# The new tokens' down product: four full-precision matmuls of 32 columns side by side, summed at the end

## What is computed

```python
D_MODEL = 1024; SEQ = 2048; DEC_SEQ = 32; D_FF = 4 * D_MODEL

def merge_and_ffn(x, oa, ob, oc, gc, onorm_c, w_o, norm_ffn, w_up, w_down):
    ...
    mixed = jnp.concatenate([...], axis=-1)
    h = x + jnp.einsum('bte,ed->btd', mixed, w_o)
    u = jax.nn.relu(jnp.einsum('btd,df->btf', rmsnorm(h, norm_ffn), w_up))
    return h + jnp.einsum('btf,fd->btd', u * u, w_down)
```

## Time and profile before

| what | value |
|---|---|
| median of 3 executions | 3143.09 us (3139.33 to 3143.40) |
| the profiled execution | 3146.91 us, of which its span (first to last instruction) 3145.2 us |
| PE busy | 2971.3 us, 94% of the span |
| DVE, ACT, POOL busy | 1645.0, 960.7, 327.9 us |
| DMA | 310 MB moved, mean 99 GB/s |
[...]
| last third of the MLP | about 2722 to 3145 us of the span |

### The profile page before, as it was taken

How to read it: one execution, slowest core, us unless ns; L and a number is a source line. 1 busy time by engine, 2 the same in 40 slices (tenths; PEclk the granted TensorE clock), 3 DMA queues, 4 the chain that set the end, 5 groups by cost and what they waited for, 6 DMA issues and landing times.

```text
span 3145.2 us, 45442 instructions
## 1 busy us (share of the span) xinstructions
PE 2971.3 (94%) x18200; PEld 2624.4 (83%) x18200; DVE 1645.0 (52%) x2241; ACT 960.7 (31%) x1621; POOL 327.9 (10%) x504
## 2 busy tenths in 40 slices
PE   6999789989999999869999999999999999999999
PEld 4678678878888899857899999888999998888887
DVE  4545244357556578863545445535544545455554
ACT  3322155545555322112322212223221222322221
POOL 1222110011000144640000000000000000000000
PEclk9999899999999999989999999999999999999999
DMA  6652322246222544323211212232121212232221
GB/s 208 191 194 99 104 79 77 71 138 175 70 85 75 160 133 145 108 92 121 94 54 62 72 54 88 89 105 81 65 70 54 81 67 109 83 108 81 81 81 42
DMA packets 280227, 310.23 MB, mean 99 GB/s; under 512 B 53036, under 2 KB 233870, under 8 KB 280018
## 3 DMA queue, kind: packets, MB, share of 16 engines
q1 hardware_dynamic: 280018, 307.33, 30.0%
HBM read 239.51 MB, written 67.78 MB: 98 GB/s over the span
## 4 chain that ended last, share of the span: by engine, by line
PE 52%; DMA 1%; DVE 1%; ACT 1%; issue 0%; SPq 0%; ACTq 0%; DVEq 0%
PE mf_psO L2058 28%; PE mf_psT L2099 22%; PE mf_psO L2099 1%; PE mf_psO L2081 1%; DMA mf_nat<-scratch_mix 1%; PE mf_psT L2044 1%; DVE mf_wlo L1945 1%; ACT mf_whi L1874 1%; DVE mf_acc L2015 0%; ACT mf_hs L1927 0%; DVE mf_acc L1968 0%; DVE mf_hs L1974 0%; SPq L1819 0%; ACT mf_xhi L1889 0%; SPq L1850 0%
## 5 line engine op out<-in xcount | busy, mean ns | idle before, releaser
L2015 DVE TENSOR_TENSOR mf_acc<-mf_psO,mf_acc 128x1024 f32<-128x1024 f32 x272 | 332.8, 1224 | 381.9 <-PE mf_psO L2058 381.6
L2099 PE MATMUL mf_psT<-mf_xhi,mf_wlo 128*128 128x384 f32 (+1 forms) x1440 | 459.3, 319 | 0.0
L2099 PE MATMUL mf_psT<-mf_xhi,mf_whi 128*128 128x384 f32 (+1 forms) x1440 | 459.2, 319 | 0.0
L2099 PE MATMUL mf_psT<-mf_xlo,mf_whi 128*128 128x384 f32 (+1 forms) x1440 | 459.2, 319 | 0.0
L2058 PE MATMUL mf_psO<-mf_whi,mf_uhi 128*128 128x512 f32 (+1 forms) x1088 | 429.1, 394 | 9.2 <-DVE mf_acc L2015 9.2
L2058 PE MATMUL mf_psO<-mf_wlo,mf_uhi 128*128 128x512 f32 (+1 forms) x1088 | 427.4, 393 | 0.0
L2058 PE MATMUL mf_psO<-mf_whi,mf_ulo 128*128 128x512 f32 (+1 forms) x1088 | 427.3, 393 | 0.0
L1874 ACT ACTIVATE mf_whi<-mf_st 128x2048 fp32r<-128x2048 f32 x108 | 206.1, 1911 | 555.3 <-PE mf_psO L2058 528.9
L2099 PEld LDWEIGHTS mf_psT<-mf_xhi,mf_whi 128*128 128x128 f32 x1440 | 270.4, 188 | 2.8
L2099 PEld LDWEIGHTS mf_psT<-mf_xlo,mf_whi 128*128 128x128 f32 x1440 | 270.3, 188 | 1.7
L2099 PEld LDWEIGHTS mf_psT<-mf_xhi,mf_wlo 128*128 128x128 f32 x1440 | 270.4, 188 | 0.0
(11 more groups left out here) (199 smaller groups left out, 5459.7 us busy)
## 6 DMA issues: line engine op xcount, KB each, us to landing
mf_st<-in_w_up SPq DMA_DIRECT2D x48, 1024.0 KB, 5.4
mf_st<-in_w_down SPq DMA_DIRECT2D x48, 1024.0 KB, 6.2
md_wst<-in_w_in SPq DMA_DIRECT2D x24, 1024.0 KB, 5.3
pj_wst<-in_w_in SPq DMA_DIRECT2D x18, 1024.0 KB, 6.7
scratch_proj<-pj_ob SPq DMA_DIRECT2D x48, 256.0 KB, 2.0
mf_st<-in_w_o SPq DMA_DIRECT2D x12, 1024.0 KB, 6.1
pj_xin<-in_x_prompt SPq DMA_DIRECT2D x16, 512.0 KB, 5.6
md_qn<-scratch_proj SPq DMA_DIRECT2D x64, 128.0 KB, 2.7
```

The costliest lines, as they stand in the source:

```text
L2015: nc.vector.tensor_tensor(acc[0:r, i, :], psO[k % 2][0:r, :], acc[0:r, i, :], ALU.add).then_inc(s["o_out"], 1)
L2099: last = nc.tensor.matmul(up_psum(t, f, b, cn), wa[b4][:, w0:w0 + P], xa[:, j, c0:c0 + cn], start=j == 0 and q == 0, stop=j == KD - 1 and ...
```

## The change

It concerns the new tokens' down product in the last third (`t == LAST`), and nothing in the first two thirds.

- **PE.** For each piece the 12 float32r matmuls of the new tokens are replaced by `new_tokens`: four matmuls on plain float32 operands, g = 0 to 3, one for each pair of hidden block and half of the output columns. Each has 32 columns of weights (the squared activations, `mf_usq`) and 512 moving columns (the unsplit weights), and writes to PSUM partitions 32g to 32g+31, so each lies in its own quarter of PE's columns. Each starts and stops its own sum, nothing is accumulated in PSUM.
- **Order.** In the last third the new tokens' product comes first in each piece, not last (`order_of`), on PE and on DVE.
- **DVE.** It copies the last 32 columns of `sq` to `usq` (one copy for each hidden block, between the square and its low part); it adds the product's 128x512 to `mf_part` in place of the add of 32x1024 to `acc`. After the last piece two adds of 32x1024 bring the four quarters into `acc` (the new tokens' rows).
- **SP.** Each w_down piece of the last third is loaded twice: unsplit into both halves of `mf_nat` (p even) or `mf_xin` (p odd), and into `mf_st` as before. The unsplit load comes first and waits for the new tokens' product of p-2 (for p = 0 and 1: for the last use of the tile before). At the end `mf_part` is moved to `mf_hs` in four DMAs of 64 KB, quarter to the new tokens' rows, before the stores; the new tokens' store comes last, after the two adds.
- **Tiles.** `nat`, `xin` and `hs` become one tile each with two halves.

```diff
+        wraw = [nat2, xin2]
+        usq = S.sb("mf_usq", [P, 2 * FP, NEW])
+        part = S.sb("mf_part", [P, 512])
+        def order_of(t, p):
+            n = len(THIRDS[t])
+            return [n - 1, *range(n - 1)] if t == LAST and p >= 0 else list(range(n))
...
             def load_piece(t, what, p):
                 m = piece(t, what, p)
+                src = piece_src(what, p)
+                if t == LAST and what == "d":
+                    if p >= 2:
+                        sp.wait_ge(s["o_done"], o_index(t, 0, p - 2) + 1)
+                    elif p == 0:
+                        sp.wait_ge(s["t_ready"], t_index(t, len(THIRDS[t]) - 1, False) + 1)
+                    else:
+                        sp.wait_ge(s["o_out"], o_index(t, len(THIRDS[t]) - 1, -1) + 1)
+                    sp.dma_start(wraw[p % 2][:, :, :], src).then_inc(raw_loaded[p % 2], 16)
                 if m >= 2:
...
+                    if t == LAST and i == 0:
+                        sp.wait_ge(s["o_out"], o_index(t, 0, NP - 1) + 1)
+                        for g in range(4):
+                            sp.dma_start(hs2[0:NEW, g // 2, (g % 2) * 512:(g % 2) * 512 + 512],
+                                         part[g * NEW:(g + 1) * NEW, :]).then_inc(gathered, 16)
...
+            sp.wait_ge(parts_ready, 2)
+            sp.dma_start(y(t0, r), acc[0:r, len(THIRDS[LAST]) - 1, :]).then_inc(stored, 16)
...
+                        if t == LAST and b == 1:
+                            if f >= 2 * FP:
+                                dve.wait_ge(s["o_done"], o_index(t, 0, f // FP - 2) + 1)
+                            nc.vector.tensor_copy(usq[:, f % (2 * FP), :], sq[k % 2][:, cn - NEW:cn]
+                                                  ).then_inc(usq_ready, 1)
                         dve.wait_ge(s["uhi_ready"], k + 1)
...
+                            if t == LAST and i == nt - 1:
+                                if p == 0:
+                                    nc.vector.tensor_copy(part[:, :], psO[k % 2][:, 0:512]).then_inc(s["o_out"], 1)
+                                else:
+                                    nc.vector.tensor_tensor(part[:, :], psO[k % 2][:, 0:512], part[:, :],
+                                                            ALU.add).then_inc(s["o_out"], 1)
+                                continue
...
+            dve.wait_ge(gathered, 16 * len(TILES[1::2]) + 64)
+            mine = acc[0:NEW, len(THIRDS[LAST]) - 1, :]
+            for j in range(2):
+                if j:
+                    dve.wait_ge(parts_ready, j)
+                nc.vector.tensor_tensor(mine, mine, hs2[0:NEW, j, :], ALU.add).then_inc(parts_ready, 1)
...
+                def new_tokens(k, p):
+                    pe.wait_ge(s["o_out"], k - 1)
+                    pe.wait_ge(usq_ready, FP * (p + 1))
+                    pe.wait_ge(raw_loaded[p % 2], RAW0 + 16 * (p // 2 + 1))
+                    for g in range(4):
+                        j, half = divmod(g, 2)
+                        last = nc.tensor.matmul(psO[k % 2][g * NEW:(g + 1) * NEW, 0:512],
+                                                usq[:, (FP * p + j) % (2 * FP), :],
+                                                wraw[p % 2][:, j, half * 512:half * 512 + 512], start=True, stop=True)
                     last.then_inc(s["o_done"], 1)
```

More of the change, by code:

```diff
@@ L1698, in merge_and_ffn @@
         mhalf = S.sb("mf_mhalf", [P, 1])
-        nat = [S.sb(f"mf_nat{i}", [P, D]) for i in range(2)]
-        xin = [S.sb(f"mf_xin{i}", [P, D]) for i in range(2)]
-        hs = [S.sb(f"mf_hs{i}", [P, D]) for i in range(2)]
+        nat2, xin2, hs2 = [S.sb(z, [P, 2, D]) for z in ("mf_nat", "mf_xin", "mf_hs")]
+        nat, xin, hs = [[z[:, i, :] for i in range(2)] for z in (nat2, xin2, hs2)]
         ss = S.sb("mf_ss", [P, len(TILES)])
@@ L1711, in merge_and_ffn @@
         ulo = S.sb("mf_ulo", [P, 2 * FP, HT], F32R)
+        wraw = [nat2, xin2]
+        usq = S.sb("mf_usq", [P, 2 * FP, NEW])
+        part = S.sb("mf_part", [P, 512])
+        LAST = NTH - 1
         rl = [hs[i][:, 0:HT // 2] for i in range(2)]
@@ L1723, in merge_and_ffn @@
         stored = S.sem("mf_stored")
+        usq_ready = S.sem("mf_usq_ready")
+        parts_ready = S.sem("mf_parts_ready")
+        raw_loaded, gathered = [nat_loaded[0], x_loaded[0]], x_loaded[1]
+        RAW0 = 16 * len(TILES[0::2])
+        def order_of(t, p):
+            n = len(THIRDS[t])
+            return [n - 1, *range(n - 1)] if t == LAST and p >= 0 else list(range(n))
         def t_index(t, i, second):
@@ L1817, in load_piece @@
                     sp.wait_ge(s["wlo_ready"], m - 1)
-                src = piece_src(what, p)
                 sp.dma_start(st[m % 2][:, :].rearrange("p (k n) -> p k n", k=src.shape[1]), src
@@ L1848, in _ @@
                         load_mixed(t + 1, i + 2)
-                    sp.wait_ge(s["o_out"], o_index(t, i, NP - 1) + 1)
+                    if t == LAST and i == len(tiles) - 1:
+                        continue
[4 more added lines that the diff above has]
+                                         part[g * NEW:(g + 1) * NEW, :]).then_inc(gathered, 16)
+                    sp.wait_ge(s["o_out"], o_index(t, order_of(t, 0).index(i), NP - 1) + 1)
                     sp.dma_start(y(t0, r), acc[0:r, i, :]).then_inc(stored, 16)
+            t0, r = TILES[-1]
+            sp.wait_ge(parts_ready, 2)
+            sp.dma_start(y(t0, r), acc[0:r, len(THIRDS[LAST]) - 1, :]).then_inc(stored, 16)
             sp.wait_ge(stored, 16 * len(TILES))
@@ L2010, in _ @@
                     if p >= 0:
-                        for i, (t0, r) in enumerate(tiles):
-                            k = o_index(t, i, p)
+                        for pos, i in enumerate(order_of(t, p)):
+                            r = tiles[i][1]
+                            k = o_index(t, pos, p)
                             dve.wait_ge(s["o_done"], k + 1)
                             dve.wait_ge(s["o_out"], k)
+                            if t == LAST and i == nt - 1:
[4 more added lines that the diff above has]
+                                                            ALU.add).then_inc(s["o_out"], 1)
+                                continue
                             nc.vector.tensor_tensor(acc[0:r, i, :], psO[k % 2][0:r, :], acc[0:r, i, :],
@@ L2085, in out_proj @@
                     last.then_inc(s["o_done"], 1)
+                def new_tokens(k, p):
[7 more added lines that the diff above has]
+                                                wraw[p % 2][:, j, half * 512:half * 512 + 512], start=True, stop=True)
+                    last.then_inc(s["o_done"], 1)
                 def up(f, b):
@@ L2125, in _ @@
                     bd = wbuf("d", p)
-                    for i, (t0, r) in enumerate(tiles):
+                    for pos, i in enumerate(order_of(t, p)):
+                        if t == LAST and i == nt - 1:
+                            new_tokens(o_index(t, pos, p), p)
+                            continue
+                        t0, r = tiles[i]
                         c = slice(t0 - base, t0 - base + r)
@@ L2132, in _ @@
                                 steps.append((ua[:, f, c], wa[bd][:, j * D:(j + 1) * D]))
-                        product(o_index(t, i, p), r, steps)
+                        product(o_index(t, pos, p), r, steps)
                         if p == NP - 1 and t + 1 < NTH and i < len(THIRDS[t + 1]):
```

## The result

The changed kernel takes 3122.14 us (median of 4, 3120.36 to 3127.81), the kernel before 3143.24 (median of 4, 3139.33 to 3147.27). The ratio is 0.9937, with a 95% interval of 0.9924 to 0.9949: 21.1 us faster, where 23.6 were forecast. The profiled execution took 3127.81 us, its span is 3126.1.

What follows compares the result with a forecast made beforehand. PE's unbroken stream was taken to bound the last third. 15 x 1.69 = 25.4 us, and 0.6 in piece 0, less 2.4 at the end, gave 23.6 us off 3143.09: 3119.5 us, range 3113 to 3123.

Steps and rivals of the forecast that it cites:

- Four quarters at once: New tokens' product: four column quarters work simultaneously as two halves do; 1.10 us a product instead of 2.79; chance 0.66.
- rounds: New tokens' product: a 512-column record takes 0.43 us; the product's eight records take two such steps, 0.86 us.
- Two at a time: Rival for the new tokens' product: the array works on only two quarters at once; range then up to 3134; chance 0.13.
- One step apart: Rival: records start strictly in program order, so four quarters take 2.35 us a product; 3138.3 us in all; chance 0.07.
- one after the other: Rival: 32-column float32 quarters don't overlap; product 3.64 us, 0.85 more than before; 3157.6 us in all; chance 0.06.
- The ends of the product: Way into and out of the new tokens' product on PE: 0.24 us together, bounds 0 and 0.25.
- The sum: Whole kernel: 15 x 1.69 = 25.4, and 0.6, less 2.4: 23.6 us less, 3119.5 us.
- drains: Term of the forecast's range: the time would be 3.8 us lower without them.
- The second weight load: Behind L1183's records: some of the 0.15 us before the next matmul, hidden by a 0.43 us round on 512 columns.
- Piece 0: Last third's first piece: PE's wait for DVE grows from 3.1 to about 4.2 us; gain 0.6 us, not 1.69.
- The loads and DVE's copies: Steady pieces: unsplit w_down load costed at nothing; two copies of about 0.1 us each, with 1.6 us of cover.
- The end: After PE's last matmul: two extra 32x1024 adds, about 1.2 us each, before the store; +2.4 us, bounds 2.0 and 3.5.

Runs made afterwards that it cites:

- in blocks: Changed kernel with two quarters only, each accumulating two hidden blocks; program order first, first, second, second. 3134.64 us, ratio 0.9967 to the kernel before.
- the set issued twice: Changed kernel with each piece's four new-token matmuls issued twice, the second set overwriting the first with the same values. 3133.47 us, ratio 0.9965 to before.
- one quarter: Changed kernel with all four matmuls of a piece in the first quarter of PE's columns, and no parts to add at the end. 3155.61 us, ratio 1.0037.
- the order alone: Kernel before, with the new tokens' 12 float32r matmuls first in each piece of the last third. 3144.57 us against 3142.55, ratio 1.0008.
- the earlier adds: Changed kernel with the two final 32x1024 adds between the last piece's 128-row adds, new tokens' store ahead of the last tile's. 3122.25 us, ratio 0.9932.
- DVE's order changed: Changed kernel; in the last third's piece 0 the two weight splits go behind DVE's first and second add. 3117.03 us, ratio 0.9918 to before.
- in turns: Changed kernel with two quarters only, each accumulating two hidden blocks; program order first, second, first, second. 3132.13 us, ratio 0.9963 to the kernel before.
- the last kernel's: Changed kernel with the final adds earlier and, in all three thirds, piece 0's splits behind DVE's first adds. 3103.31 us, ratio 0.9875 to before.

## Why the prediction was right

**Four quarters at once: right.** The step that carried the forecast went from two halves in the earlier trace rows to four quarters. The trace has four records under way, and the runs with one, two and four quarters have products of 3.76, 2.07 and 1.20 us: each doubling of quarters halves the rounds. "Two at a time" (0.13 in the forecast) would be four rounds of 0.44 us and 0.32 us at the ends, 2.08 us, which is what two quarters take; four take 1.20. No run shows a limit below four. "One step apart" and "one after the other" are refuted too; the last was priced 3157.6 and the run that forces it gave 3155.61. The run that forces "one after the other" has no adds at the end, which the price counted with 2.4 us, so its total agrees in part by luck; the product itself was priced at 3.64 and took 3.76. Of a strict program order across quarters no sign is left: with the quarters in blocks, a record of the second quarter must be under way while earlier ones of the first wait. What lets it pass them the runs don't show.

**The ends of the product: the size was off.** The sum took 0.24 us for both ends; they cost 0.32 (by the set issued twice), and a round is 0.44 us, not 0.43. What was missing is 0.10 us behind the first matmul after the group, whose successor comes 0.33 us later in place of 0.23. That makes 1.59 us a piece in place of 1.69, 1.5 us in all.

What the ends are is shown in part only. The forecast's range counts 3.8 us (16 x 0.24) for drains, but no run shows a drain; the runs show 0.32 us for both ends of a product. On the way in it is 0.08 to 0.10 us ahead of plain float32 matmuls of 32 or 64 columns (here, with one quarter, on L1183), and none ahead of those of all 128 columns on L1143 (388.30 - 388.12 = 0.18, the spacing of the matmuls ahead). It isn't the 32 columns alone: the float32r product of 32 columns starts without delay, 0.13 us after the last up matmul in the run with the order alone, and 0.22 in the earlier trace rows. The 0.10 us behind the group is another matter. It comes as well behind plain float32 matmuls of all 128 columns, where the number of columns doesn't change: on L667 after L1156 in the kernel before, 0.26 us between the first two matmuls, then 0.18. So it goes with the step from plain float32 back to float32r, and L667 pays it where no column groups are used. The second weight load, to which the prediction puts some of the 0.15 us behind L1183's records, no run takes apart; a weight load is 0.14 us long there, with rounds of 0.11, and 0.11 on L2147, with rounds of 0.44.

```profile
389.73 0.42 PE L667 MATMUL md_psD<-xhi,md_whi 128*128 128x384 f32 x1
389.99 0.33 PE L667 MATMUL md_psD<-xlo,md_whi 128*128 128x384 f32 x1
390.17 0.34 PE L667 MATMUL md_psD<-xhi,md_wlo 128*128 128x384 f32 x1
```

**Piece 0: the mechanism right, the clock left to chance.** The wait grew as worked out, from 2.93 to 3.95 us. But the sum left the stretch at the lower clock as it was, and that stretch differs between executions. In the changed kernel's profiled execution 4.8 us of work went by at the lower level, against 3.4 before, and that ate the rest: piece 0 takes 18.51 us, 0.1 less than before (18.58), not 0.6 less. In the run with the earlier adds, with the same program here and the same wait, it was 3.4 us and piece 0 took 17.85, 0.7 less than before: there the term comes out as forecast. With one execution of each, the term stands somewhere between 0.1 and 0.7. That the wait and the clock behind it make piece 0 long is shown by the run with DVE's order changed.

**The last piece but one: not foreseen.** At 3107.63 the chain goes through an add of DVE. The piece before the last has no up product behind it, so the new tokens' product follows a 128-row tile directly. It is now shorter (1.0 us) than DVE's add of that tile (1.24 us), and the product after it waits for that add, 0.32 us:

```profile
3107.52 1.07 PE L2147 MATMUL mf_psO<-mf_xin,mf_usq 128*32 128x512 f32 x8
3108.91 0.50 PE L2112 MATMUL mf_psO<-mf_whi,mf_uhi 128*128 128x512 f32 x1 [0.32 <-DVE mf_acc L2063]
```

In the steady pieces the up products lie between, and nothing waits.

**The loads and DVE's copies: right.** PE waits for no load in the steady pieces, ACT's split is released by PE. The second load costs nothing. DVE's copies take 0.18 us each, and are hidden. The added DMA traffic is 17 MB (310 to 327).

**The end: right.** 2.4 us forecast, 2.4 measured.

**The sum.** 15 x 1.59 = 23.9, less 0.3 for the wait before the last piece, plus 0.1 in piece 0, less 2.4 at the end: 21.3 us. The medians say 21.1, and so do the traces from the start of piece 0's down products to the end (397.1 us before, 376.0 after). The 2.3 us that the forecast was too high are 1.5 at the ends of the products, 0.5 in piece 0 and 0.3 for the wait not foreseen. The two profiled executions differ by 19.1 only, since the changed one reached the last third 2.0 us later, in stages that the change doesn't touch.

## What to carry to other kernels

A product that fills a quarter of PE's columns is cheap to speed up if independent parts of it can be written to different column groups: here 12 matmuls in one quarter took 2.79 us, and four slower ones side by side 1.20, of which 0.32 is at the two ends, so such products should come in sets as large as can be. Test the extreme case (all parts in one group) to see whether it is the placement or the rewriting that pays; here the rewriting alone was a loss of 1 us a piece. And look at where the engine that the product feeds is busy with something else: a faster product in front of a stalled add only lengthens the stall, and a few lines that put the adds ahead of the splits were worth 5 to 6 us a third in the traces.

## What the runs showed of the hardware that was not expected

- Column groups take their matmuls independently of program order, at least across the four records of two matmuls: in blocks or in turns, 1.85 and 1.84 us in the chain.
- The same wait is followed by different stretches of the lower clock, or by none. In the first two thirds, where nothing was changed, PE waits 3.13 us in piece 0 in every trace but the last kernel's. In two of them (one quarter; two quarters in turns, both in the first third) the granted clock then stays at 1.00 and the down products take 19.8 us; in most it is at 0.50 for 3.4 us, and they take 21.2 to 21.4; in two (the change; the order alone, both in the second third) for 6.8 us, part of it within the wait, and they take 22.5 and 22.6. In the kernel without the wait they take 16.5 in both thirds. So the wait's length doesn't settle what follows it, and one trace doesn't price it; only without the wait was piece 0 the same each time. The spread of 3 us between executions may come from there in part, which was not tried apart.
- The 0.10 us between plain float32 and the float32r matmuls behind it is paid whether or not column groups are used: on L667 above 0.26 us in place of 0.18, and with one, two and four quarters 0.34, 0.33 and 0.33 in place of 0.23.
